# Moving every large SBUF buffer of a two-block transformer kernel to a 512-byte boundary

## The chip, the cores and the metric

The kernel runs on one core of one Trainium2 chip. The metric is device time in microseconds (us) from the start to the end of one launch; a lower time is better. All data is fp32 in HBM. The kernel keeps everything on one core: five engines (TensorE, VectorE, ScalarE, GpSimd, SyncE) run their own instruction lists and meet through semaphores, and transfers are issued from SyncE's queue (SP) and, a few, from ScalarE's.

## The reference: two transformer blocks on 256 tokens

The first block takes 256 tokens and 16 meta tokens of width 1024, mixes them (latent attention with 8 heads beside a short gated convolution), and sends them through a two-level mixture of experts. The second block mixes with pooling and windowed attention, and ends in a dense gated layer of width 2816.

```python
def hier_moe(h, ...):                      # 4 groups x 8 experts, each 1024 -> 256 -> 1024
    g_w, g_idx = lax.top_k(g_prob, 1)      # one group for each token
    e_w, e_idx = lax.top_k(e_prob, TOP_K)  # two experts of it
    ...
    a = jnp.einsum('nd,edf->nef', t, w_gate)
    b = jnp.einsum('nd,edf->nef', t, w_up)
    hid = jax.nn.silu(a) * b * combine[:, :, None]
    routed = jnp.einsum('nef,efd->nd', hid, w_down)
    shared = (jax.nn.silu(t @ w_sh_gate) * (t @ w_sh_up)) @ w_sh_down
    return (routed + shared).reshape(bsz, slen, d)

def second_block(x, ...):
    ...
    u = rms_norm_2(h, norm_ffn[l])
    h = h + (jax.nn.silu(u @ w_ffn_gate[l]) * (u @ w_ffn_up[l])) @ w_ffn_down[l]
    return rms_norm_2(h, norm_final)
```

## The kernel before

**The weight stream.** All weights lie in HBM as one list of entries of 128 partitions x 2048 fp32 (`SLOT`), 1 MiB each; an entry brings each partition one row of 8192 bytes. SyncE loads them in the order of their use. Most go to `ring`, a circle of 8 places of 8192 bytes per partition. While the circle would not be enough, some go "aside": `home(n)` sends them to `work`, `turned_w`, `yields`, `beside` or `extra`. Two runs of entries do so: 12 at first, and later 8 more (the entries from `AGAIN_AT` to `AGAIN_END`), of which six lie in `work` and two in `turned_w`. After these 8 all loads go to `ring`.

**What holds a load back.** Before SyncE issues a load it waits until the place is free: on the semaphore `used` or `split_used`, which TensorE raises when it has read the entry that lay there. Each place has a semaphore of its own (`full`) that the landed load raises.

**The stages.** From the start to about 120 us comes the first block's mixing, in which most weights are first split: ScalarE copies an entry to `single` in a rounded form (line 404, `w_hi`), VectorE subtracts this from the entry and writes the rest back into its place (line 411, `ring_r`), and TensorE multiplies three times instead of once. Then comes routing, and from about 140 to 345 us the experts: 4 groups of 8, each in 24 entries (twice 8 of gate and up, 4 of down), read by TensorE without a split, straight from where they landed. From about 345 us the second block follows, with split weights again; its gated layer takes the time from about 490 us to the end. Nearly all matrix products go through one helper, `mm` on line 1637; transposes go through line 1640.

**Where the buffers lie.** The program's allocator gives each tensor the next multiple of 32 bytes behind the one before it; the first free byte is 1121. Only `work` is put at a multiple of 512 by hand. So the starting bytes within each partition are, before the change:

```
buffer     bytes   start    start mod 512
ring       65536    1152    128
h           8192   66688    128
cst         9112   74880    128
vec         3612   84000     32
extra      16384   87616     64
stat         640  104000     64
gain        4096  104704    256
single     32768  108800    256
turned     17408  141568    256
work       69632  159232      0
```

Each place of `ring` is 16 x 512 bytes, so all 8 begin 128 bytes behind a multiple of 512. `yields` and `beside` lie inside `single` and `gain` at whole multiples of 512 from `gain`'s start, so at 256 behind one. `ring_r`, `extra_r`, `turned_w` and `work_r` are other names for the same bytes.

Of the kernel before, what the change touches and what calls it, by code (L numbers as in the profile page):

```python
# [17 lines left out]
F32 = mybir.dt.float32  # L18
F32R = mybir.dt.float32r
# [5 lines left out]
P = 128  # L25
D = 1024
DT = D // P
TOK = 256
NT = TOK // P
META = 16  # L30
COLS = META + TOK
# [26 lines left out]
SLOTS = 8  # L58
SLOT = 2048
WORK = 17408  # L60
# [17 lines left out]
ASIDE, ASIDE_WORK, EXTRA = 12, 6, 2  # L78
# [22 lines left out]
CN = C_QS + CT  # L101
# [16 lines left out]
VN = V_PG + 4 * P  # L118
# [9 lines left out]
def two_blocks(nc, x, meta, consts, small, gains, positions, stream, out):  # L128
    ctx = ExitStack()
    with ctx:  # L130
        def sb(name, shape, dt=F32):
            return ctx.enter_context(nc.sbuf_tensor(name, shape, dt))
# [2 lines left out]
            return ctx.enter_context(nc.semaphore(name))  # L135

        ring = sb("ring", [P, SLOTS, SLOT])
        ring_r = nc.alloc_sbuf_tensor_at("ring_r", [P, SLOTS, SLOT], F32R, offset=nc.sbuf_base - 4 * SLOTS * SLOT)
        h = sb("h", [P, NT, D])  # L140
        cst = sb("cst", [P, CN])
        vec = sb("vec", [P, VN])
        extra = sb("extra", [P, EXTRA, SLOT])
        extra_r = nc.alloc_sbuf_tensor_at("extra_r", [P, EXTRA, SLOT], F32R, offset=nc.sbuf_base - 4 * EXTRA * SLOT)
        stat = sb("stat", [P, 160])
        pos_i = sb("pos_i", [P, NT], I32)
        rounds_i = sb("rounds_i", [P, 2], I32)

        gain = sb("gain", [P, D])
        beside_at = nc.sbuf_base - 4 * D
        single = sb("single", [P, 4 * SLOT], F32R)
        assert nc.sbuf_base == beside_at + 4 * (D + 4 * SLOT)
        beside = nc.alloc_sbuf_tensor_at("beside", [P, SLOT], F32, offset=beside_at)
        yields = nc.alloc_sbuf_tensor_at("yields", [P, SLOT], F32, offset=nc.sbuf_base - 4 * SLOT)
        turned = sb("turned", [P, 2, DT * COLS], F32R)
        turned_w = nc.alloc_sbuf_tensor_at("turned_w", [P, 2 * DT * COLS], F32, offset=nc.sbuf_base - 4 * 2 * DT * COLS)

        def halved(a, n, w):  # L160
            return a[:, 0:n * w].rearrange("p (a b) -> p a b", b=w)
# [12 lines left out]
        w_hi = [single[:, b * SLOT:(b + 1) * SLOT] for b in range(HIGHS)]  # L174

        work_at = -(-nc.sbuf_base // 512) * 512
        work = nc.alloc_sbuf_tensor_at("work", [P, WORK], F32, offset=work_at)
        work_r = nc.alloc_sbuf_tensor_at("work_r", [P, WORK], F32R, offset=work_at)
        top = [0]  # L180

        def cut(*shape, dt=F32):
# [2302 lines left out]
```

## Time and profile before

| | us |
|---|---|
| median of 3 runs | 679.77 (678.7 to 680.94) |
| the profiled execution, device time | 678.28 |
| its span, first to last instruction | 676.5 |
| TensorE matmuls busy | 628.6 (93%) |
| VectorE busy | 356.1 (53%) |
| ScalarE busy | 293.0 (43%) |
| GpSimd busy | 52.3 (8%) |
| HBM read | 179.04 MB, 266 GB/s over the span with the writes |

A share of busy time is a mean over stages with different limits, and a pipelined matmul counts as busy while it waits for another. So the share says little by itself; the chain of waits says which work ended last in each stretch, and the windows say how fast the transfers ran there.

### The profile page before, as it was taken

The page shows a single profiled execution, that of the slowest core. Times are in us where ns is not written, and L with a number is a line of the kernel's source. Part 1 is how long each engine was busy: PE and PEld are TensorE (multiplying, and loading weights), DVE is VectorE, ACT ScalarE, POOL GpSimd, SP SyncE. Part 2 cuts the span into 40 slices and gives each one's busy share as a digit, 9 for nine tenths or more (in the row PEclk, how much of TensorE's full clock was granted, in tenths as well). Part 3 has the DMA queues.
Part 4 walks back from the last instruction along what each step waited for, and adds up shares of the span by engine and source line. Part 5 has one row for each costly group of instructions (what it writes and reads, how often), then busy time and mean ns, then how long its engine had stood idle before and what let it go on. Part 6 is the DMA issues. An engine that isn't in the chain of part 4 may idle for free.

```text
span 676.5 us, 10104 instructions
## 1 busy us (share of the span) xinstructions
PE 628.6 (93%) x3973; PEld 471.5 (70%) x3973; DVE 356.1 (53%) x689; ACT 293.0 (43%) x561; POOL 52.3 (8%) x75
## 2 busy tenths in 40 slices
PE   8999899999999756779899999999999999999996
PEld 5979788842543311333379999897788888888884
DVE  5687664731130120110087898657866666666665
ACT  6855562421111110100085675555655555555554
POOL 3100101100010000000044700000100000000001
PEclk9999999999999997788999999999999999999999
DMA  8956338999999999999997533354545555555101
GB/s 345 420 229 249 120 131 327 417 366 425 425 386 420 423 419 422 421 422 420 421 422 313 186 126 126 139 179 182 187 153 192 197 198 193 187 188 187 63 0 63
DMA packets 26286, 180.73 MB, mean 267 GB/s; under 512 B 3184, under 2 KB 3312, under 8 KB 5120
## 3 DMA queue, kind: packets, MB, share of 16 engines
q1 hardware_dynamic: 25200, 177.60, 66.3%
q10 hardware_dynamic: 1040, 2.50, 0.9%
q8 instruction: 32, 0.52, 0.3%
q14 instruction: 14, 0.11, 0.1%
HBM read 179.04 MB, written 1.05 MB: 266 GB/s over the span
## 4 chain that ended last, share of the span: by engine, by line
PE 70%; DMA 16%; DVE 7%; ACT 4%; issue 2%; SPq 0%; POOLq 0%; POOL 0%; ACTq 0%; DVEq 0%
PE ps L1637 67%; DMA ring<-stream_dram 15%; PE ps L1640 3%; DVE ring_r L411 2%; ACT single L404 1%; DMA h<-x_dram 1%; DVE work L1572 1%; ACT work L905 1%; DVE work L1575 1%; DVE h L1625 0%; DVE work L1628 0%; ACT turned L910 0%; DVE work L1448 0%; ACT work L806 0%; DVE turned L1111 0%
## 5 line engine op out<-in xcount | busy, mean ns | idle before, releaser
L1637 PE MATMUL ps<-turned,single 128*128 128x256 f32 (+2 forms) x960 | 234.1, 326 | 1.6 <-ACT work L676 0.8
L1637 PE MATMUL ps<-turned,ring_r 128*128 128x256 f32 (+1 forms) x656 | 182.0, 281 | 0.0
L1637 PEld LDWEIGHTS ps<-turned,single 128*128 128x128 f32 x960 | 158.7, 189 | 18.6 <-issue 2.0
L411 DVE TENSOR_TENSOR ring_r<-ring,single 128x1024 fp32r<-128x1024 f32 (+1 forms) x132 | 160.2, 1236 | 14.6 <-ACT single L404 14.4
L404 ACT ACTIVATE single<-ring 128x1024 fp32r<-128x1024 f32 (+1 forms) x132 | 134.1, 1047 | 0.1
L1637 PEld LDWEIGHTS ps<-turned,ring_r 128*128 128x128 f32 x656 | 122.6, 188 | 0.4
L1637 PE MATMUL ps<-ring,work 128*32 128x512 f32 (+2 forms) x462 | 70.0, 612 | 16.9 <-DMA ring<-stream_dram 14.8
L1637 PEld LDWEIGHTS ps<-single 128*128 128x128 f32 x257 | 38.7, 190 | 34.1 <-issue 21.1
L1637 PE MATMUL ps<-single 128*128 128x512 f32 (+1 forms) x257 | 55.8, 356 | 2.9 <-DVE single L1459 1.9
L1637 PE MATMUL ps<-single,turned 128*128 128x512 f32 (+2 forms) x176 | 53.9, 382 | 3.1 <-DVE turned L1247 1.6
L1637 PE MATMUL ps<-single,work_r 128*128 128x512 f32 x176 | 56.2, 392 | 0.0
L1637 PEld LDWEIGHTS ps<-ring,work 128*32 128x32 f32 (+1 forms) x462 | 19.9, 119 | 50.0 <-issue 23.7
L1605 DVE TENSOR_TENSOR work<-work,ps 128x512 f32<-128x512 f32 x22 | 15.1, 687 | 60.1 <-ACT work L935 60.1
L1637 PE MATMUL ps<-work 128*128 128x128 f32 (+6 forms) x240 | 42.7, 399 | 3.0 <-DVE work L1105 1.8
L935 ACT ACTIVATE work<-ps 128x512 f32<-128x512 f32 x22 | 13.2, 600 | 73.1 <-PE ps L1637 73.1
L813 ACT ACTIVATE work<-ps 128x256 f32<-128x256 f32 x8 | 3.1, 384 | 90.9 <-PE ps L1637 90.9
L1459 DVE SCALAR_TENSOR_TENSOR single<-ps,work,single 128x512 fp32r<-128x512 f32 x16 | 12.0, 751 | 53.5 <-ACT single L819 53.5
L1448 DVE TENSOR_TENSOR work<-work,ps 128x256 f32<-128x256 f32 x8 | 3.4, 421 | 69.7 <-ACT work L813 69.7
L1637 PEld LDWEIGHTS ps<-single,turned 128*128 128x128 f32 (+1 forms) x176 | 31.2, 180 | 10.9 <-DVE ring_r L411 2.8
L1637 PE MATMUL ps<-ring,turned_w 128*32 128x512 f32 x208 | 30.5, 697 | 8.3 <-DMA ring<-stream_dram 5.7
L1637 PEld LDWEIGHTS ps<-single,work_r 128*128 128x128 f32 x176 | 33.0, 187 | 7.3
L1039 POOL TENSOR_SCALAR stat<-stat 128x1 f32<-128x1 f32 (+1 forms) x7 | 4.7, 666 | 422.3 <-ACT ps L950 177.7
(261 smaller groups left out, 733.8 us busy)
## 6 DMA issues: line engine op xcount, KB each, us to landing
ring<-stream_dram SPq DMA_DIRECT2D x145, 1024.0 KB, 12.0
work<-stream_dram SPq DMA_DIRECT2D x12, 1024.0 KB, 12.1
turned_w<-stream_dram SPq DMA_DIRECT2D x4, 1024.0 KB, 14.0
extra<-stream_dram SPq DMA_DIRECT2D x2, 1024.0 KB, 11.1
ring<-stream_dram SPq DMA_DIRECT2D x2, 832.0 KB, 8.1
h<-x_dram SPq DMA_DIRECT2D x2, 512.0 KB, 4.7
gain<-gains_dram ACTq DMA_DIRECT2D x2, 512.0 KB, 10.6
yields<-stream_dram SPq DMA_DIRECT2D x1, 1024.0 KB, 12.5
```

Of the source, the lines that this page charges most:

```text
L404: act.activation(w_hi[k % HIGHS][:, a], ring[:, place, a], ACT.Copy).then_inc(s["whi_done"], 1)
L411: dve.tensor_tensor(ring_r[:, place, a], ring[:, place, a], w_hi[k % HIGHS][:, a].bitcast(F32), ALU.subtract).then_inc(s["wlo_done"], 1)
L905: act.activation(gate[:, m, :], gate[:, m, :], ACT.Sigmoid).then_inc(s["sig_done"], 1)
L935: act.activation(fpart[:, m % 2, :].rearrange("p (a b) -> p a b", b=TOK), ffn_banks(m)[:, :, TOK:2 * TOK], ACT.Copy).then_inc(s["fsg_done" ...
L1039: pool.tensor_scalar(ms, ss, 1.0 / D, EPS, ALU.mult, ALU.add).then_inc(s["pool_step"], 1)
L1448: dve.tensor_tensor(htok, sg, ps[:, 4, FF:2 * FF], ALU.mult).then_inc(s["ht_done"], 1)
L1459: dve.scalar_tensor_tensor(yl[:, n * 512:(n + 1) * 512], ps[:, 6 + n, :], wsl[:, p:p + 1], yh[:, n * 512:(n + 1) * 512].bitcast(F32), ALU. ...
L1572: dve.tensor_tensor(gate[:, m, :], gate[:, m, :], ps[:, 2 + m % 4, :], ALU.mult).then_inc(s["br_sb"], 1)
L1575: dve.tensor_tensor(gate[:, m, 0:TOK], gate[:, m, 0:TOK], gate[:, m, TOK:2 * TOK], ALU.add).then_inc(s["mg_sum"], 1)
L1605: dve.tensor_tensor(halves(fsum[:, m % 2, :], TOK), halves(fpart[:, m % 2, :], TOK), ffn_banks(m)[:, :, 0:TOK], ALU.add).then_inc(s["fh_su ...
L1637: return pe.matmul(o, lhsT, rhs, start=start, stop=stop, **kw)
L1640: return pe.transpose(o, a, ident[0:rows, 0:rows])
```

## The change

Only where buffers lie is changed. No instruction, wait or transfer is added, removed or moved in order. The small tiles (`stat`, `pos_i`, `rounds_i`) are allocated first. Then a helper `placed` puts the large buffers one behind the other from the next multiple of 512; their sizes are all whole multiples of 512, so each begins at one. The constants `cst` and `vec` come last.

```diff
-        ring = sb("ring", [P, SLOTS, SLOT])
-        ring_r = nc.alloc_sbuf_tensor_at("ring_r", [P, SLOTS, SLOT], F32R, offset=nc.sbuf_base - 4 * SLOTS * SLOT)
-        h = sb("h", [P, NT, D])
-        cst = sb("cst", [P, CN])
-        vec = sb("vec", [P, VN])
-        extra = sb("extra", [P, EXTRA, SLOT])
...
+        LINE = 512
+        where = [-(-nc.sbuf_base // LINE) * LINE]
+
+        def placed(name, shape, dt=F32):
+            n = 4
+            for d in shape[1:]:
+                n *= d
+            at = where[0]
+            where[0] += n
+            return nc.alloc_sbuf_tensor_at(name, shape, dt, offset=at), at
+
+        ring, ring_at = placed("ring", [P, SLOTS, SLOT])
+        ring_r = nc.alloc_sbuf_tensor_at("ring_r", [P, SLOTS, SLOT], F32R, offset=ring_at)
+        h, _ = placed("h", [P, NT, D])
+        extra, extra_at = placed("extra", [P, EXTRA, SLOT])
...
+        gain, beside_at = placed("gain", [P, D])
+        single, single_at = placed("single", [P, 4 * SLOT], F32R)
...
+        turned, turned_at = placed("turned", [P, 2, DT * COLS], F32R)
...
+        work, work_at = placed("work", [P, WORK])
+        work_r = nc.alloc_sbuf_tensor_at("work_r", [P, WORK], F32R, offset=work_at)
+        cst, cst_at = placed("cst", [P, CN])
+        where[0] = -(-where[0] // 32) * 32
+        vec, _ = placed("vec", [P, VN])
```

By these lines the starts become: `stat` 1152, `ring` 2048, `h` 67584, `extra` 75776, `gain` 92160, `single` 96256, `turned` 129024, `work` 146432, `cst` 216064 (all but `stat` multiples of 512) and `vec` 225184 (416 behind one).

## Rows read from the trace of the kernel before

**Rows 1.** The page: span in 40 slices (clock, GB/s), and the chain by line

```profile
PEclk9999999999999997788999999999999999999999
...
GB/s 345 420 229 249 120 131 327 417 366 425 425 386 420 423 419 422 421 422 420 421 422 313 186 126 126 139 179 182 187 153 192 197 198 193 187 188 187 63 0 63
...
PE ps L1637 67%; DMA ring<-stream_dram 15%; PE ps L1640 3%; DVE ring_r L411 2%; ACT single L404 1%; DMA h<-x_dram 1%; DVE work L1572 1%; ACT work L905 1%; DVE work L1575 1%; DVE h L1625 0%; DVE work L1628 0%; ACT turned L910 0%; DVE work L1448 0%; ACT work L806 0%; DVE turned L1111 0%
```

**Rows 2.** Chain of waits, 100 to 360 us: start, length, what set the time

```profile
204.59 13.52 DMA ring<-stream_dram
...
219.82 19.06 DMA ring<-stream_dram
...
310.55 17.61 DMA ring<-stream_dram
```

**Rows 3.** Windows: stretch, busy PE, PEld, DVE, ACT, POOL (x), clock, DMA share, GB/s

```profile
108.00:133.00 25.00, 24.45 (x137) 20.28 (x136) 17.32 (x44) 9.18 (x20) 5.06 (x9) 1.00 1.01 426
160.00:190.00 30.00, 27.60 (x192) 14.31 (x188) 3.59 (x6) 3.83 (x8) 0.00 (x0) 1.00 1.01 427
177.00:189.00 12.00, 12.00 (x70) 7.04 (x71) 0.69 (x1) 0.84 (x2) 0.00 (x0) 1.00 1.01 425
190.00:206.00 16.00, 15.48 (x130) 6.45 (x126) 5.27 (x14) 2.14 (x4) 2.40 (x3) 1.00 0.96 376
206.00:218.00 12.00, 11.16 (x54) 4.05 (x46) 0.42 (x1) 1.46 (x3) 0.00 (x0) 1.00 1.01 425
228.00:328.00 100.00, 76.58 (x457) 27.45 (x455) 11.23 (x25) 8.95 (x18) 0.00 (x0) 0.88 1.01 421
```

**Rows 4.** Timeline of SP's queue, 100 to 345 us: start, length, issues

```profile
151.30 5.03 SPq L587 DMA_DIRECT2D work<-stream_dram  x5
156.85 2.45 SPq L587 DMA_DIRECT2D turned_w<-stream_dram  x2
159.83 0.33 SPq L587 DMA_DIRECT2D work<-stream_dram  x1
164.52 40.39 SPq L598 DMA_DIRECT2D ring<-stream_dram  x15
```

**Rows 5.** DMA issues of 228 to 328 us: size, median us to landing

```profile
ring<-stream_dram SPq DMA_DIRECT2D x41, 1024.0 KB, 17.7
```

**Rows 6.** TensorE groups by form, 100 to 204 us: total busy, mean ns

```profile
L1637 PE MATMUL ps<-ring,turned_w 128*32 128x512 f32 x48 | 5.6, 594 | 0.5 <-ACT turned_w L815 0.5
L1637 PE MATMUL ps<-work,turned_w 128*32 128x512 f32 x40 | 4.7, 595 | 0.7 <-DVE work L1439 0.7
```

**Rows 7.** Groups by form, 500 to 660 us, all engines

```profile
L411 DVE TENSOR_TENSOR ring_r<-ring,single 128x1024 fp32r<-128x1024 f32 x58 | 70.0, 1221 | 0.0
...
L1637 PEld LDWEIGHTS ps<-turned,ring_r 128*128 128x128 f32 x316 | 59.4, 188 | 0.4
L1637 PEld LDWEIGHTS ps<-turned,single 128*128 128x128 f32 x316 | 59.3, 188 | 13.2
...
L1605 DVE TENSOR_TENSOR work<-work,ps 128x512 f32<-128x512 f32 x21 | 14.4, 687 | 59.9 <-ACT work L935 59.9
...
L1610 DVE TENSOR_TENSOR work<-work 128x256 f32<-128x256 f32 x20 | 8.5, 425 | 0.7
```

**Rows 8.** Timeline of weight loads, 318 to 332 us, with idle time before each

```profile
321.39 0.16 PEld L1637 LDWEIGHTS ps<-ring,work 128*32 128x32 f32 x8 [0.37 <-issue]
...
323.51 0.16 PEld L1637 LDWEIGHTS ps<-ring,work 128*32 128x32 f32 x8 [0.37 <-DMA ring<-stream_dram]
...
325.72 0.16 PEld L1637 LDWEIGHTS ps<-ring,work 128*32 128x32 f32 x8 [0.46 <-DMA ring<-stream_dram]
...
328.21 0.16 PEld L1637 LDWEIGHTS ps<-ring,work 128*32 128x32 f32 x8 [0.73 <-DMA ring<-stream_dram]
```

**Rows 9.** Window of the longest low clock

```profile
299.00:308.00 9.00, 8.48 (x42) 3.87 (x38) 1.74 (x6) 1.19 (x3) 0.00 (x0) 0.50 1.01 420
```

**Rows 10.** Tile ring, 228 to 328 us, TensorE: ns min/median/max

```profile
L1637 PE MATMUL ps<-ring,work x232: 592/612/1061, 228.2 to 326.2; 128*32 128x512 f32 x116
```

More of the change, by code:

```diff
@@ L135, in sem @@
             return ctx.enter_context(nc.semaphore(name))
-        ring = sb("ring", [P, SLOTS, SLOT])
-        ring_r = nc.alloc_sbuf_tensor_at("ring_r", [P, SLOTS, SLOT], F32R, offset=nc.sbuf_base - 4 * SLOTS * SLOT)
-        h = sb("h", [P, NT, D])
-        cst = sb("cst", [P, CN])
-        vec = sb("vec", [P, VN])
-        extra = sb("extra", [P, EXTRA, SLOT])
-        extra_r = nc.alloc_sbuf_tensor_at("extra_r", [P, EXTRA, SLOT], F32R, offset=nc.sbuf_base - 4 * EXTRA * SLOT)
         stat = sb("stat", [P, 160])
@@ L147, in two_blocks @@
         rounds_i = sb("rounds_i", [P, 2], I32)
[L151 to L154, printed above, removed]
-        beside = nc.alloc_sbuf_tensor_at("beside", [P, SLOT], F32, offset=beside_at)
-        yields = nc.alloc_sbuf_tensor_at("yields", [P, SLOT], F32, offset=nc.sbuf_base - 4 * SLOT)
-        turned = sb("turned", [P, 2, DT * COLS], F32R)
-        turned_w = nc.alloc_sbuf_tensor_at("turned_w", [P, 2 * DT * COLS], F32, offset=nc.sbuf_base - 4 * 2 * DT * COLS)
+        LINE = 512
[11 more added lines that the diff above has]
+        extra, extra_at = placed("extra", [P, EXTRA, SLOT])
+        extra_r = nc.alloc_sbuf_tensor_at("extra_r", [P, EXTRA, SLOT], F32R, offset=extra_at)
+        gain, beside_at = placed("gain", [P, D])
+        single, single_at = placed("single", [P, 4 * SLOT], F32R)
+        assert single_at == beside_at + 4 * D
+        beside = nc.alloc_sbuf_tensor_at("beside", [P, SLOT], F32, offset=beside_at)
+        yields = nc.alloc_sbuf_tensor_at("yields", [P, SLOT], F32, offset=single_at + 4 * 3 * SLOT)
+        turned, turned_at = placed("turned", [P, 2, DT * COLS], F32R)
+        turned_w = nc.alloc_sbuf_tensor_at("turned_w", [P, 2 * DT * COLS], F32, offset=turned_at)
+        work, work_at = placed("work", [P, WORK])
[3 more added lines that the diff above has]
+        vec, _ = placed("vec", [P, VN])
         def halved(a, n, w):
@@ L174, in two_blocks @@
         w_hi = [single[:, b * SLOT:(b + 1) * SLOT] for b in range(HIGHS)]
-        work_at = -(-nc.sbuf_base // 512) * 512
-        work = nc.alloc_sbuf_tensor_at("work", [P, WORK], F32, offset=work_at)
-        work_r = nc.alloc_sbuf_tensor_at("work_r", [P, WORK], F32R, offset=work_at)
         top = [0]
```

## The prediction

> **What bounds the kernel now.** I read the page first. Its chain gives TensorE's line 1637 about two thirds of the span and the loads into `ring` 15%; VectorE and ScalarE have a few per cent [rows 1]. The GB/s line shows where the loads matter: slices 13 to 21 run at 419 to 425 without a gap, and on both sides the rate falls to 120 to 200 [rows 1]. So a new placement has two doors: the transfers, in the expert stage, and the engines, everywhere else.
>
> Then the chain of waits between 100 and 360 us. Up to 204 us it is TensorE with some VectorE. From 204.59 us on, the loads into `ring` set the time: six pieces from 204.59 to 328.16 us, of which the first, the second and the last stand here; between them TensorE and the others have 1 to 12 us at a time [rows 2]. In 228 to 328 us the DMA share is 1.01, with 41 loads issued 17.7 us ahead of their landing [rows 3, 5]. At 1 MiB per 2.49 us (1,048,576 bytes at 421 GB/s) that is some seven loads queued: what counts in this stretch is how fast the DMA engines write, not when SyncE issues. After 345 us TensorE is the bound to the end.
>
> The windows then give the clue. SyncE's queue has one stretch in which eight loads in a row go elsewhere than to `ring`: five to `work`, two to `turned_w`, one to `work`, issued from 151.30 to 160.16 us [rows 4]. Landing takes up to about 19 us, so they move at about 158 to 178 us. `work` starts at a multiple of 512 bytes already, `turned` at one of 256. The window 160 to 190 shows 427 GB/s and 108 to 133 (in which also most loads go aside) 426; 228 to 328, in which every load goes to `ring`, 128 bytes behind a multiple, shows 421 [rows 3]. One thing speaks against reading this as the price of the offset: the first loads to `ring` after the eight are as fast, 425 in 177 to 189, and so is 206 to 218, behind a gap, also 425 [rows 3]. I read these as the engines' own buffering: if writing is slower than reading by 1.2%, a DMA engine needs some loads until its buffer is full and the read has to wait. That every fast `ring` stretch stands behind aligned loads or behind a gap (190 to 206 moved only 376 GB/s) fits. It is an inference, and the experiments would have to show it.
>
> **The change part by part.** No instruction, wait or DMA is added or removed, so there are only prices that move.
>
> *Loads into ring.* The stretch bound by them lasts 328.2 - 204.6 = 123.6 us; its first 13 us run at 425 already, so 110 us at 421 are left. At the aligned rate of 426 (the window of 25 us; 427 and 425 stand beside it) they take 110 x 421/426 = 108.7 us: 1.3 us less. Lower bound: 0, if alignment isn't what separates the rows. Upper bound: all 123.6 us from 421 to 427 give 1.7 us, and the whole fast stretch free of its small gaps perhaps 2.2 (an estimate: 428 and 429 would be one GB/s or two above any long window). Before 204 us the same loads are faster too, but TensorE's own work sets the time there, and hides it: 12.00 us busy of 12 in 177 to 189, 15.48 of 16 in 190 to 206 [rows 3]. In 190 to 206 a place comes free only when TensorE has read it, so nothing queued earlier helps.
>
> *How much of the 1.3 us reaches the end.* Here TensorE comes in. Its clock is at 0.50 in 299 to 308 us [rows 9], and matmuls take up to 1061 ns there instead of 592 [rows 10]. So it falls behind the loads and afterwards catches up: its step for one load is 323.51 - 321.39 = 2.12 us against the loads' 2.49 [rows 8]. It first waits for a load again at 323.51 us; the idle time beyond the usual 0.37 is 0.09 us at 325.72 and 0.36 at 328.21 [rows 8]. If TensorE's work stood still in time, only 0.45 us could be gained at 328 us. But TensorE began this stretch behind an earlier wait for a load, near 298 us, by when some 0.9 us of the 1.3 have been gained (80 of 110 us); half of it or more survives the low clock, whose end need not move. So TensorE's path gains 0.45 + (0.45 to 0.9) = 0.9 to 1.35 us and the loads' path 1.3; the later one counts. I take 1.2 us.
>
> *After 328 us.* TensorE is the bound and all 1.2 us go through to the end; loads run at half the share there, and a faster load is worth nothing.
>
> *Engines.* What does an operand cost at another offset? TensorE: 512 columns moved from `ring` (offset 128) and from `work` (offset 0) cost 594 and 595 ns [rows 6]; weight loads from `ring_r` (128) and `single` (256) cost 188 and 188 [rows 7]. VectorE: 256 elements in `work` alone take 425 ns and 512 take 687, 262 more per 256; on that line 1024 elements would be 1211, and line 411, whose operands lie at 128 and 256, takes 1221 [rows 7]. I cost all engine work at nothing. Bounds: 10 ns on each of 132 instructions of line 411, 1.3 us of VectorE, which has idle time in every stage; at most 0.3 us of it on the chain, which gives that line 2%. ScalarE's and GpSimd's accesses get the same zero by the same likeness. The small tiles and `vec` stay at multiples of 32 but not of 512; only columns of them are read.
>
> *Start and end.* The chain gives `h` from `x` 1%, about 6 us [rows 1]. At 1.2% of that, 0.07 us; zero.
>
> **Sum.** The profiled execution took 678.28 us, a span of 676.5 and 1.8 around it; it becomes 676.5 - 1.2 + 1.8 = 677.1. It lies 0.2% below the median of the runs, so I forecast 679.77 - 1.2 = 678.6 us. I call 0.3% (2.0 us) the limit of what a measurement of this kernel can tell from no change; the forecast lies within it.
>
> **Rivals.**
>
> *Alignment does nothing for the loads (0.17).* The time stays 679.8. For it: fast stretches with `ring` loads exist. It would be so if reads from HBM set 421 and the fast stretches had another reason. The Trainium skill (SBUF — State Buffer, "A bandwidth-pool intuition that's wrong") takes HBM's share of a core, about 358 GB/s, for the end-to-end limit, by which the writing side could not matter. The rows run at 421 to 427, so that figure doesn't bind in this trace.
>
> *The gain is larger than the bounds of the rows (0.20).* Over 2.0 us, some 677.0: alignment takes away also what the 426 GB/s windows still contain, or line 411 and TensorE gain a few ns each that these rows don't separate. 0.25% of the 348 us behind 328 us would be 0.9 us more. Against it: the same durations at three offsets.
>
> *Slower: a stretch of low clock falls into work that TensorE bounds (0.10).* The low stretch of 10 us at 299 us costs nothing now, as the loads cover it. Were it to come at 330 us or later, it would cost 9 us x (1 - 592/1061) = 4.0 us, less 1.2: 682.6 us. It takes 3.2 us of net loss (a low stretch of over 7 us) to show as slower. For it: the clock falls after stretches of idle TensorE, and faster loads move these in time. Against it: TensorE's idle share in 228 to 328 hardly changes (23% to 22%), and the page shows full clock in all slices from 19 on [rows 1].
>
> **How the numbers follow.** The forecast of 678.6 has 0.53, with a range of its own from 677.8 to 679.8. The shown runs spread over 2.2 us, so a median may miss by 1 us in any case. Faster by over 0.3%: the larger gain, and a little of the forecast's upper tail, 0.22. Slower: 0.11. Within: 0.67. The range from 676.3 to 681.0 leaves out half of the slower case and the tail of the larger gain.
>
> **What would show it.** The window of the 100 us in which all loads go to `ring` should read 425 to 427 GB/s instead of 421; if it stays at 421, the step of the loads fails. The loads' pieces of the chain should still set the time from about 205 to about 327 us; the piece behind should start some 1.2 us earlier. Line 411 should stay at 1221 ns, weight loads at 188, the matmuls of the expert stage at 592; if one moves by over 1%, the step of the engines fails, and TensorE's would decide, as it bounds 348 us. If the span moves by several us while all these stand, look at where the low clock fell.

## The result: slower by 0.25%, with faster loads

| | us |
|---|---|
| changed kernel, median of 22 runs | 680.76 (678.78 to 682.6) |
| kernel before, timed beside it, median of 22 | 678.85 (677.64 to 680.94) |
| ratio, 95% interval | 1.0025 (1.0016 to 1.0035) |
| profiled execution, device time and span | 679.79, 678.0 |

By the bound of 0.3% this is no clear change, but the interval leaves out 1: the kernel became some 1.7 us slower (0.25% of 679; 1.1 to 2.4 us by the interval), and I had forecast 1.2 us faster. The windows of the changed kernel (columns as in [rows 3]) show that the loads did what was forecast:

```profile
108.00:133.00 25.00, 24.42 (x139) 20.45 (x138) 17.52 (x45) 9.17 (x20) 5.05 (x9) 1.00 1.00 420
160.00:190.00 30.00, 27.61 (x190) 14.29 (x186) 3.89 (x7) 3.82 (x8) 0.00 (x0) 1.00 1.01 428
...
206.00:218.00 12.00, 11.26 (x54) 4.07 (x50) 0.81 (x2) 1.45 (x3) 0.00 (x0) 1.00 1.01 424
228.00:328.00 100.00, 76.77 (x462) 28.32 (x454) 11.58 (x26) 9.23 (x19) 0.00 (x0) 0.88 1.01 427
329.50:332.90 3.40, 3.40 (x12) 0.89 (x11) 0.00 (x0) 0.00 (x0) 0.00 (x0) 0.50 1.01 429
```

The 100 us in which every load goes to `ring` run at 427 GB/s where they ran at 421 [rows 3]. Short windows are coarse. An estimate: if the packets of 8192 bytes of the 16 DMA engines end nearly together, a window holds one round of 131,072 bytes more or less, which is 5 GB/s over 25 us and 1.3 over 100. Only the long window is proof. The window of 108 to 133 us, from which the forecast took its 426 as the aligned rate, reads 420 in both profiles of the changed kernel, with every load aligned. So it was no measure of that rate; that 427 came out in the long window does not rest on it.

The longest pieces of the changed kernel's chain of waits (start, length, what set the time), and behind them the two in the expert stage:

```profile
173.62 17.59 PE ps L1645 x112
...
307.80 18.43 DMA ring<-stream_dram
346.80 27.03 PE ps L1645 x220
486.63 181.01 PE ps L1645 x954
```

```profile
326.28 1.11 PE ps L1645 x8
...
329.22 9.71 PE ps L1645 x46
```

The same pieces of the kernel before:

```profile
173.91 17.59 PE ps L1637 x112
...
331.15 8.15 PE ps L1637 x46
347.18 26.93 PE ps L1637 x220
486.90 179.24 PE ps L1637 x954
```

At the end of the loads the changed kernel is 328.21 - 326.28 = 1.93 us ahead [rows 2, 8]. By 347 us only 0.38 is left, as a stretch of low clock (0.50 in 329.5 to 332.9) makes the next TensorE piece last 9.71 us instead of 8.15. And the gated layer, one piece of 954 matmuls, lasts 181.01 us instead of 179.24: 1.77 us that nothing in the forecast allows for. It begins 0.27 us earlier (486.63 against 486.90) and so ends 1.5 us later, which is the difference of the spans (678.0 against 676.5). The piece of 220 and the work between the two grew too, by 0.1 us each. So from the start of the piece of 220 to the end of the span it is 331.2 us instead of 329.3.

The groups by form of that stage (500 to 660 us; busy, mean ns), first before, then changed:

```profile
L1637 PE MATMUL ps<-turned,single 128*128 128x512 f32 x317 | 110.5, 392 | 0.0
L1637 PE MATMUL ps<-turned,ring_r 128*128 128x256 f32 x317 | 89.0, 281 | 0.0
L1637 PE MATMUL ps<-single,work_r 128*128 128x512 f32 x147 | 47.1, 391 | 0.0
L1637 PE MATMUL ps<-ring_r,work_r 128*128 128x512 f32 x73 | 28.4, 389 | 0.0
```

```profile
L1645 PE MATMUL ps<-turned,single 128*128 128x512 f32 x315 | 110.7, 396 | 0.0
L1645 PE MATMUL ps<-turned,ring_r 128*128 128x256 f32 x314 | 87.7, 279 | 0.0
L1645 PE MATMUL ps<-single,work_r 128*128 128x512 f32 x144 | 46.6, 394 | 0.0
L1645 PE MATMUL ps<-ring_r,work_r 128*128 128x512 f32 x72 | 28.4, 394 | 0.0
...
L419 DVE TENSOR_TENSOR ring_r<-ring,single 128x1024 fp32r<-128x1024 f32 x58 | 70.1, 1221 | 0.0
...
L1645 PEld LDWEIGHTS ps<-turned,ring_r 128*128 128x128 f32 x314 | 59.2, 188 | 0.4
```

VectorE's 1221 ns and the weight loads' 188 are the old ones [rows 7], and the fastest matmuls of the expert stage take 592 ns as before [rows 10]. The matmuls of 512 columns take 3 to 5 ns more, those of 256 take 2 less. All four kinds belong to one stream without idle time, so the piece of the chain is the better measure of its pace, and I use it below.

### The profile page after: what moved, and what is told of

It reads as the page before. It is cut to its first block, busy times and chain, and to the rows that moved or that the text cites. A ratio compares the mean times of both kernels' runs of the same rounds, so it can differ in the third digit from the quotient of the medians.

```text
span 678.0 us, 10104 instructions
## 1 busy us (share of the span) xinstructions
PE 631.1 (93%) x3973; PEld 473.3 (70%) x3973; DVE 356.3 (53%) x689; ACT 292.7 (43%) x561; POOL 52.2 (8%) x75
## 4 chain that ended last, share of the span: by engine, by line
PE 71%; DMA 15%; DVE 7%; ACT 4%; issue 2%; ACTq 0%; POOLq 0%; SPq 0%; POOL 0%; DVEq 0%
PE ps L1645 68%; DMA ring<-stream_dram 14%; PE ps L1648 3%; DVE ring_r L419 2%; ACT single L412 1%; DMA pos_i<-positions_dram 1%; DVE work L1580 1%; ACT work L913 1%; DVE work L1583 1%; DVE h L1633 0%; DVE work L1636 0%; ACT turned L918 0%; DVE work L1456 0%; ACT work L814 0%; DVE turned L1119 0%
## 5 line engine op out<-in xcount | busy, mean ns | idle before, releaser
L1645 PE MATMUL ps<-ring,turned_w 128*32 128x512 f32 x208 | 28.9, 667 | 7.5 <-DMA ring<-stream_dram 5.0
```

The lines of the kernel that those rows point to most:

```text
L1645: return pe.matmul(o, lhsT, rhs, start=start, stop=stop, **kw)
```

## The experiments

All kernels are the changed one with a gap in front of some buffers. The helper gets an argument, and each experiment names buffers and the distance behind a multiple of 512 at which they start; buffers not named start at a multiple (`vec` at one of 32).

```diff
-        def placed(name, shape, dt=F32):
+        def placed(name, shape, dt=F32, behind=0):
+            where[0] += (behind - where[0]) % LINE
...
-        vec, _ = placed("vec", [P, VN])
+        vec, _ = placed("vec", [P, VN], behind=where[0] % LINE)
```

**First question: does the slower gated layer come from the placement, and from which buffers?** Engine buffers back, `ring` aligned:

```diff
-        extra, extra_at = placed("extra", [P, EXTRA, SLOT])
+        extra, extra_at = placed("extra", [P, EXTRA, SLOT], behind=64)
...
-        turned, turned_at = placed("turned", [P, 2, DT * COLS], F32R)
+        turned, turned_at = placed("turned", [P, 2, DT * COLS], F32R, behind=256)
```

(`gain` and `single` likewise at 256.)

> The changed kernel, but extra, gain, single and turned begin again where they did modulo 512 (64 and 256); ring and h stay at multiples of 512. Theory A (the transfers care for the offset of ring, TensorE's pace in the gated layer for the offset of the buffers that it reads, above all single and turned): loads at 427 GB/s in 228 to 328 us and the last long TensorE piece of the chain back at 179.2 us instead of 181.0; 1 to 2 us faster than the kernel before, some 677.5 us. Theory B (that piece is longer because ring moved too, or by chance of the execution): it stays at 181 us, and the time stays 1 to 2 us above the kernel before. Theory C (only where the low clock falls counts): the piece is the same in all four runs.

Measured: 680.36 us, ratio 1.0023 (1.0008 to 1.0038), loads at 427, and

```profile
486.90 181.01 PE ps L1646 x954
```

Theory A, that the old places of `single` and `turned` bring the old pace back, falls; its other half, that the loads go by the offset of `ring`, stands. Next, `ring` and `h` at 128 again and all others aligned:

```diff
-        ring, ring_at = placed("ring", [P, SLOTS, SLOT])
+        ring, ring_at = placed("ring", [P, SLOTS, SLOT], behind=128)
...
-        h, _ = placed("h", [P, NT, D])
+        h, _ = placed("h", [P, NT, D], behind=128)
```

> The changed kernel, but ring and h at 128 behind a multiple of 512, all other buffers at multiples. Theory A: loads back at 421 GB/s in 228 to 328 us, the last long TensorE piece of the chain at or near 181.0 us; slower than the changed kernel by 1 us or so, or as slow as it where the low clock takes the gain anyway: 681 to 682 us. Theory B: loads at 421 GB/s and the piece at 179.2 us, the time that of the kernel before.

Measured: 678.51 us, ratio 0.999 (0.9981 to 1.0), loads at 421, and

```profile
489.40 179.09 PE ps L1646 x954
```

So `ring` and `h`, moved from 128 behind a multiple of 512 to one, do both: they make the loads faster and the gated layer slower (a run below takes `ring` alone). Second profiles of both kernels, unchanged, to see what repeats:

> The changed kernel once more, for a second profile. If the 181.0 us of the last long TensorE piece come from the placement, they repeat within 0.3 us; if from the execution, they may be 179 here. The loads run at 427 GB/s. Where the clock stands low may differ; if a low stretch falls behind 328 us again, the gain of the loads is again gone by 347 us.

> The kernel before once more, for a second profile. 421 GB/s, and the last long TensorE piece at 179.2 us within 0.3 if the placement sets it. Where the clock stands low may differ from the first profile; the span follows it by 1.5 us for each 3.4 us of low clock behind 328 us.

```profile
486.77 180.98 PE ps L1645 x954
```

```profile
486.67 179.19 PE ps L1637 x954
```

(First the changed kernel, then the one before.) The piece repeats within 0.05 us, so it is no chance of an execution. Where the clock stands low differs from profile to profile: the low stretch at 329.5 us wasn't there in the changed kernel's second profile, and its matmuls of 331 to 339 us took 8.13 us.

At the piece of 220 that second profile is only 0.16 us ahead of the kernel before (346.89 against 347.05). But it had begun its first long TensorE piece 1.95 us later than the other (15.78 against 13.83), so the loads' gain is there. The pieces of 112 and of 46 matmuls, which stand at the two ends of the expert stage, first of the changed kernel's second profile, then of the other's:

```profile
175.05 17.59 PE ps L1645 x112
...
330.88 8.13 PE ps L1645 x46
```

```profile
173.58 17.60 PE ps L1637 x112
...
331.03 8.15 PE ps L1637 x46
```

From the start of one to the start of the other it is 155.83 us against 157.45, 1.62 less; in the first pair it is 155.60 against 157.24, 1.64 less. What a low clock does to this depends on where it falls. At 307.6 us it made TensorE set the time from there to 329 us, and the 1.62 us were gained all the same; at 329.5 us it took 1.56 of the 1.64 back. The window of that low clock, and the piece of the chain:

```profile
307.60:311.00 3.40, 3.40 (x12) 1.44 (x13) 0.75 (x1) 0.69 (x1) 0.00 (x0) 0.50 1.00 424
```

```profile
307.53 21.52 PE ps L1645 x112
```

**Second question: is it the place of ring, or its distance to the others?** `ring` aligned, all others (`extra`, `gain`, `single`, `turned`, `work`) at 128:

> ring and h at multiples of 512; extra, gain, single, turned and work 128 behind one. Theory P (phase: TensorE's pace in the gated layer falls when the buffers that it reads side by side, ring_r beside single, turned and work, lie in the same phase, and 128 bytes of distance avoid it): the last long TensorE piece is 179.2 us again, the loads stay at 427 GB/s in 228 to 328 us, and the time is below both kernels, 677 to 678 us. Theory R (what counts is where ring itself lies, a multiple of 512 being slow for TensorE and fast for the loads): the piece stays at 181.0 us, loads at 427, time 680 us.

Measured: 677.97 us, ratio 0.9991 (0.9978 to 1.0005). Window and chain:

```profile
228.00:328.00 100.00, 74.98 (x470) 27.51 (x470) 11.23 (x25) 8.95 (x18) 0.00 (x0) 0.91 1.01 427
```

```profile
486.29 179.19 PE ps L1646 x954
```

`ring` lies at a multiple of 512, and the gated layer keeps its old pace. The time is not clearly below the kernel before, but 0.34% below the changed one (0.9991 against 1.0025; each was compared with the kernel before). The reverse, all at 128, and again timed:

> All large buffers 128 behind a multiple of 512, so all in one phase. Theory P: the last long TensorE piece is 181.0 us. Theory R: 179.1. The loads into ring run at 421 GB/s by both.

> All large buffers 128 behind a multiple of 512, timed: the slow loads and the shared phase together. If both costs add, it takes the kernel before plus 2 us or slightly more (680.6 to 681.2 us). If the faster loads of the changed kernel were themselves what made it slower (by moving the low clock), it takes 679.5 or less.

```profile
486.87 180.67 PE ps L1646 x954
```

```profile
490.36 181.10 PE ps L1646 x954
```

Timed: 681.35 us (7 runs), ratio 1.0034 (1.0022 to 1.0046), the highest of all, though its interval overlaps the changed kernel's, with loads at 421. It is 2.3 us above the kernel before, so the two costs add, slightly above what I had foreseen. None of the buffers that the loads and TensorE use here lies at a multiple of 512, and the layer is slow. How the buffers lie relative to each other counts, not the place of `ring`.

These two runs also bear on the doubt that the prediction had named, the fast stretches in which `ring` was loaded at 128 [rows 3]. The window of 160 to 190 us in the two profiles:

```profile
160.00:190.00 30.00, 27.59 (x190) 14.28 (x186) 4.18 (x7) 3.83 (x8) 0.00 (x0) 1.00 1.01 421
```

```profile
160.00:190.00 30.00, 27.59 (x197) 13.52 (x195) 3.31 (x5) 3.83 (x8) 0.00 (x0) 1.00 1.01 421
```

In 177 to 189 us, by when nearly all loads go to `ring`, they read 421 and 419. The four profiles with `ring` at 128 and the other places aligned read 426 or 427 in 160 to 190 us and 425 to 428 in 177 to 189. So the same loads into `ring` at 128 ran faster behind aligned loads than behind offset ones, as far as windows this short can say.

The next two runs have `ring` alone at 128 (`h` aligned), and `ring` at 256:

> ring alone 128 behind a multiple of 512, h and all others at multiples. If ring and not h made the difference in the run with both at 128: last long TensorE piece 179.1 us, 421 GB/s. If h: 181.0 us with 421 GB/s.

> ring 256 behind a multiple of 512, all others at multiples. If 256 bytes are the unit of the loads, they run at 427 GB/s in 228 to 328 us; if 512, at 421. For TensorE: Theory P with a phase of 512 bytes, and Theory R: last long TensorE piece 179.1 us, which with 427 GB/s gives 677 to 678 us; a phase of 256 bytes: 181.0 us and 680 us.

```profile
228.00:328.00 100.00, 76.58 (x465) 28.23 (x464) 11.22 (x25) 8.94 (x18) 0.00 (x0) 0.88 1.01 421
```

```profile
486.13 179.09 PE ps L1646 x954
```

```profile
228.00:328.00 100.00, 74.84 (x466) 27.71 (x458) 11.23 (x25) 8.95 (x18) 0.00 (x0) 0.90 1.01 427
```

```profile
488.42 181.01 PE ps L1646 x954
```

(Window and chain of `ring` alone at 128, then of `ring` at 256.) So it is `ring` and not `h`; and 256 bytes apart is as bad as 0. The window of 100 us shows 421 with `ring` at 128 and 427 with it at 256, so for the loads too 256 is as good as 512. The second was timed: 679.95 us, ratio 1.0017 (1.0003 to 1.0031). Both effects are the same at 256 as at 0 and differ at 128; so far as these points go, what counts is the start modulo 256.

**Third question: which pair of buffers?** `single` (with `gain`) alone at 128, then `turned` and `work` at 128, then all but `ring` and `h` at 64:

> Only gain and single lie 128 behind a multiple of 512; ring, turned and work lie at multiples. So in the gated layer ring_r and turned share a phase, and single is apart from all. Theory P1 (what counts is that ring_r and single, used one after the other as the two halves of a weight, lie apart): last long TensorE piece 179.2 us. Theory P2 (what counts is that ring_r lies apart from the other operand of the same matmul, turned or work): 181.0 us.

> turned and work lie 128 behind a multiple of 512, ring and single at multiples: each split matmul has its two operands in different phases. P2: the piece is at most 179.2 us, perhaps less, since now the matmuls with single have distance too, and with 427 GB/s the time is 677 to 678 us. P1: 181.0 us and 680 to 681 us, as with the changed kernel.

> All but ring and h lie 64 behind a multiple of 512. If 64 bytes are distance enough for TensorE: last long TensorE piece 179.2 us; if not: 181.0. Loads into ring at 427 GB/s; those into work now start off a multiple of 256, so 160 to 190 us should show 421 to 425.

```profile
484.67 181.83 PE ps L1646 x954
```

```profile
484.78 179.91 PE ps L1646 x954
```

```profile
485.50 180.72 PE ps L1646 x954
```

None gives what either theory foresaw. `single` alone apart has the slowest piece of all placements, 181.83, though distance was added and none taken away. `turned` and `work` apart together give 179.91: between. With 64 bytes the piece is 180.72, 0.3 below the changed kernel's; the two profiles with all at 128 differ by 0.43, so this alone shows little. The window of 160 to 190 us reads 425 there, inside the range that I had given. The second was timed: 678.1 us, ratio 0.9981 (0.9968 to 0.9993), the only placement whose interval lies below 1. Three more took the pairs apart, under a theory that the price splits into one of gate and up and one of down: `work` alone, `turned` alone, and `single` with `turned`, each at 128:

> Only work lies 128 behind a multiple of 512. Theory Q (in the gated layer the price is set per kind of matmul: gate and up by the phases of ring, single and turned, down by those of ring, single and work, and the two add): down as in the run with turned and work at 128, gate and up as in the changed kernel, so the last long TensorE piece is 179.6 us (179.2 + 0.9 - 0.5). Theory S (the sum does not split so): 181.0. With loads at 427 GB/s Theory Q gives 678 us or a little less.

> Only turned lies 128 behind a multiple of 512. Theory Q: gate and up as in the run with turned and work at 128 (1.2 us above the kernel before), down as in the changed kernel (1.0 above): piece 181.4 us. Theory S: 179.9 or less, as in that run.

> gain, single and turned lie 128 behind a multiple of 512, ring and work at multiples. Theory Q: gate and up as in the kernel before (0), down as in the run with single alone at 128 (1.1 us above): piece 180.3 us. Theory S: 179.2, as in the run with work at 128 too.

```profile
487.21 180.86 PE ps L1646 x954
```

```profile
487.65 181.37 PE ps L1646 x954
```

```profile
488.67 180.63 PE ps L1646 x954
```

`turned` alone (181.37) and `single` with `turned` (180.63) are near the split's numbers (181.4 and 180.3), but `work` alone gave 180.86 where the split says 179.6. Its matmuls of gate and up, which do not read `work`, got slower too:

```profile
L1646 PE MATMUL ps<-turned,single 128*128 128x512 f32 x315 | 111.4, 398 | 0.0
L1646 PE MATMUL ps<-turned,ring_r 128*128 128x256 f32 x315 | 88.3, 280 | 0.0
```

They take 398 and 280 ns against 396 and 279 in the changed kernel, while the matmuls that read `work` fell to 392 and 390 from 394. So a price per pair, or per kind of matmul, is not the whole of it. `work` alone was timed at 679.75 us, ratio 1.0009 (0.9994 to 1.0025).

All placements in one table (start modulo 256; piece of 954 matmuls; time from the start of the piece of 220 to the end of the span; loads in 228 to 328 us; `extra` and `gain` have no column):

```
                      ring  single  turned  work   piece us        220 to end     GB/s  ratio to before
before                 128     0       0      0    179.24, 179.19  329.3, 329.2   421   1
ring and h             128     0       0      0    179.09          329.2          421   0.999
ring alone             128     0       0      0    179.09          329.2          421   -
others at 128            0   128     128    128    179.19          329.2          427   0.9991
turned and work          0     0     128    128    179.91          329.8          427   0.9981
single and turned        0   128     128      0    180.63          330.8          427   -
others at 64             0    64      64     64    180.72          330.1          427   -
work alone               0     0       0    128    180.86          331.1          427   1.0009
changed                  0     0       0      0    181.01, 180.98  331.2, 331.2   427   1.0025
engines back             0     0       0      0    181.01          331.2          427   1.0023
ring at 256              0     0       0      0    181.01          331.2          427   1.0017
all at 128             128   128     128    128    180.67, 181.10  330.9, 331.4   421   1.0034
turned alone             0     0     128      0    181.37          331.3          427   -
single alone             0   128       0      0    181.83          331.4          427   -
```

The pieces between 180.63 and 181.10 can't be put in an order by one profile each. The wider stretch adds something: with the others at 64 it is 330.1 us, 1.1 less than in the changed kernel, though the gated layer gained only 0.3; the rest was gained before that layer. And with `turned` and `work` at 128 it is 0.6 us longer than with all others at 128. So the lowest ratio, 0.9981, is not explained by the chain. It is the best of seven timed experiments, its interval overlaps that of the others at 128, and part of it may be chance.

**What the spread of the times is.** The times of each timed kernel spread over 2.7 to 5.3 us. Part of it is made in the first 16 us. The chain's first TensorE pieces, first in the second profile of the kernel before, then in the second profile with all at 128:

```profile
1.83 3.92 PE ps L1637 x6
5.75 1.85 PE ps L1640 x18
```

```profile
1.83 4.53 PE ps L1646 x6
6.36 3.09 PE ps L1649 x17
```

The six matmuls take 3.8 to 4.5 us in the profiles that show them, and the transposes behind them 1.74 to 2.18 us in ten profiles and 3.09 in five. The granted clock reads 1.00 in both of these profiles there, so it does not tell them apart. A single profile moves by up to 2 us from this, in the kernel before as in others, and by another 1.56 us if a low clock meets work that TensorE bounds. The 22 runs of the changed kernel lie in two groups of 11, 678.8 to 680.0 and 681.5 to 682.6 us, and the median stands in the empty space between. Their mean is 1.7 us above the mean of the kernel before (680.73 against 679.06), as the ratio says. A step of 2 us at the start would make such groups; that it did is not shown, as only one of these runs has a profile.

## Why the prediction was wrong, step by step

**Loads into ring: right in kind, the rate as stated.** Forecast 425 to 427 GB/s for 421, measured 427; and every placement with `ring` at a multiple of 256 shows 427, every other 421 (11 and 6 profiles). The doubt that I had named, fast stretches with offset loads, has an answer in part. With all buffers at 128 the window of 160 to 190 us fell to 421 in both profiles, and that of 177 to 189 to 421 and 419. So what was loaded before does carry over into these stretches, as the reading by buffers that fill would have it. These windows are short, and such a buffer itself was not seen. The rule of the Trainium skill (DMA: Bandwidth & Descriptors, "How a descriptor splits into AXI transactions") on starts off a multiple of 256 bytes speaks of reads, and the runs agree with it for these writes: 256 does as well as 512 and 128 does not, and the 1.6% that I had estimated from it stands beside a measured 1.4% (427/421).

**How much of it reaches the end: 1.2 us forecast, 0 to 1 found.** The stage gave what was forecast. From the start of the piece of 112 matmuls (near 174 us) to that of 46 (near 330) it is 157.5 us in the mean of the 6 profiles with loads at 421 (156.4 to 158.1) and 156.2 in the mean of the 11 with 427 (155.5 to 157.4): 1.25 us less. A part went behind it. In 3 of the 11 (the changed kernel's first, engines back, `turned` alone) a low clock made the piece of 46 last 9.71 us instead of 8.15, and in none of the 6; so at the piece of 220 the means are 0.8 us apart. Counted from the first piece of 132 matmuls to the piece of 220, it is 333.3 us in the mean of 6 (332.1 to 334.7) and 332.3 in the mean of 11 (330.9 to 333.9), 1.0 us, with single profiles up to 1.6 us from the mean of their group. The timed runs say less: with `ring` apart from the others, fast loads against slow make 0.9991 against 0.999, nothing; in one phase with them 1.0025 against 1.0034, 0.6 us; each ratio is known only to between 0.001 and 0.0014. The step named the right limit and a size that the expert stage bears out. What it put at nothing is the low clock behind 328 us: on the mean of 11 profiles it took 0.4 us (3 x 1.56 / 11). Whether the faster loads bring it there stays open, as 3 of 11 against none of 6 can be chance.

**Engines at nothing: the step that failed.** "I cost all engine work at nothing" rested on rows in which buffers at offsets 0, 128 and 256 cost the same. They do: VectorE's line 411 stayed at 1221 ns and the weight loads at 188. But all these rows are of one placement, in which `ring` happened to lie 128 bytes apart from all that TensorE reads beside it, and the others, at 0 and 256, in one phase. Rows of one placement show what each buffer costs in it. What it costs to bring them into one phase, they can't show. I had even set the point from which TensorE would decide, over 1% on the matmuls; the matmuls of 512 columns moved by about 1% (392 to 396 ns, 391 to 394, 389 to 394). The bounds for this step (1.3 us of VectorE, 0.3 on the chain) left TensorE out. It measured 1.8 us in the gated layer and 1.9 to 2.0 from the piece of 220 to the end. By the timed pairs the shared phase costs 1.0025 - 0.9991 = 0.34%, 2.3 us, with fast loads, and 1.0034 - 0.999 = 0.44%, 3.0 us, with slow ones, each known to a little over 1 us. In the timed ratios the sum is -0.6 (0.9991) + 2.3 = +1.7 us; this must come out at the measured difference, as it is made of the same ratios, and so it proves nothing. The profiles give a sum of their own: -0.8 us up to the piece of 220 and +2.0 behind it make +1.2, within the 1.1 to 2.4 us of the timed runs.

**The rivals.** None of the three is what happened. The one on the other side, a low clock in work that TensorE bounds, was seen in the profiled execution (1.56 us at 329 us) and was absent in the second profile of the same kernel, whose gated layer is as slow. It adds to single runs, some 0.4 us on the mean of the profiles with fast loads, and is not what made the kernel slower. That alignment does nothing for the loads is refuted (427 against 421 GB/s). A price for TensorE was named only as an upside of "a few ns each"; it came with the other sign.

**Range and chances.** The median lies inside the range of 676.3 to 681.0, near its upper end, and within 0.3% as the likeliest case had it, but with the sign reversed beyond its interval. That it lies inside is luck: a gain of the forecast size and a cost of 2 us that the sum did not have came together.

**Readings and sums that were wrong beside this.** The rate on the near side of the stretch of slices 13 to 21 does not fall to 120 to 200; slices 8 to 12 read 366 to 425 [rows 1]. The full clock stands from slice 20 on and not from 19. To show as slower takes 2.0 us of net loss, and it is the gross loss that is 3.2 us. VectorE's 425 and 687 ns, from which the cost of 1024 elements was drawn out, are of two lines, one of which also reads PSUM (`ps`) [rows 7]. None of these made the sign; the comparison for VectorE still came out, as line 411 did not move.

**Left open.** Why TensorE's stream is slower when the starts agree modulo 256, and which sets are slow: `single` alone apart costs more than all in one phase (181.83 against 180.67 to 181.10). The table gives the sets and their prices; neither the operands of one matmul nor the kinds of matmul explain it alone, since moving `work` changed matmuls that do not read it. VectorE and ScalarE work beside TensorE in the same buffers, and no run here took them away.

## What to carry to other kernels

Alignment is two questions: where a buffer starts for the transfers that fill it, and how it lies relative to the others that an engine streams with it. Here 256-byte starts gave the loads 1.4%, and a shared phase took 1% of a TensorE-bound layer; keeping the destination of the loads aligned and moving all engine buffers away by 128 bytes has both in the profile, while moving `single` alone made the layer slower still (181.8 against 181.0 us). In time that placement beat the changed kernel, but not clearly the kernel before (0.9991, 0.9978 to 1.0005). And rows from one placement, however equal, bound nothing about another: for a change of placement try the cost of each engine from both sides before it is set to zero.

## What the runs showed of the hardware that I had not expected

- A TensorE stream of split fp32 matmuls took 179.1 to 181.8 us depending on the starts of the buffers modulo 256, with the same instructions, no idle time, and weight loads at 187 to 189 ns. The pace repeats within 0.05 us from run to run in two of the placements, and within 0.43 in a third.
- 128 bytes between `ring` and all the others gave back all of the 1.8 us in the gated layer, 256 bytes none. 64 bytes gave back 0.3 of it, and 1.1 of 2.0 us counted from the piece of 220 to the end (one profile). 128 bytes between `single` and all the rest cost 0.8 us more.
- Transfers of 8192-byte rows ran at 421 GB/s with the destination 128 bytes behind a multiple of 256 and at 427 at one, whether or not it was a multiple of 512. Behind aligned loads, offset ones still ran at 426 to 427 in a window of 30 us that they shared; behind offset ones it read 421.
- The time before the first piece of 132 matmuls is 13.7 to 15.8 us for the same work. The first six matmuls take 3.8 to 4.5 us and the transposes behind them 1.7 to 2.2 or 3.09 us, at a granted clock that reads 1.00 in both cases.
